# One hardware loop over the two layers of the second block, with both layers on 528 columns

## The reference, cut to what matters

```
h = concat(meta, x)                     # 16 + 512 tokens
for l in range(2):
    u    = rms_norm(h, norm1_g[l])
    z    = u @ w_in[l]                  # conv, latent attention, recurrence, 3 gates of width 1024
    a    = conv_module(z)               # causal convolution with 31 taps, layer norm
    b    = mla(z)                       # 8 heads, causal attention over 528 tokens
    c    = hgrn(z)                      # gated recurrence, 4 heads
    mix  = g0*(a@Wa) + g1*(b@Wb) + g2*(c@Wc)
    h    = h + mix @ w_out[l]
    v    = rms_norm(h, norm2_g[l])
    h    = h + relu(v @ w_ff1[l])**2 @ w_ff2[l]
return h[16:]                           # the meta tokens are dropped
```

## Time and profile before

| | |
|---|---|
| time, median of three | 2974.8 us |
| profiled execution, time | 2974.41 us |
| profiled execution, span from the first to the last instruction | 2972.6 us |
| instructions | 43610 |
| PE busy | 2765.5 us, 93% |
| DVE busy | 1307.1 us, 44% |
| ACT busy | 960.5 us, 32% |
| POOL busy | 916.2 us, 31% |
| mean granted PE clock | 0.950 of full speed |
| first layer of the second block | from 873.7 us of the span |
| second layer | from 1930.9 us of the span |

### The profile page before, as it was taken

How to read it: one execution, slowest core, us unless ns; L and a number is a source line. 1 busy time by engine, 2 the same in 40 slices (tenths; PEclk the granted TensorE clock), 3 DMA queues, 4 the chain that set the end, 5 groups by cost and what they waited for, 6 DMA issues and landing times.

```text
span 2972.6 us, 43610 instructions
## 1 busy us (share of the span) xinstructions
PE 2765.5 (93%) x16664; PEld 2397.2 (81%) x16664; DVE 1307.1 (44%) x2019; ACT 960.5 (32%) x1520; POOL 916.2 (31%) x396
## 2 busy tenths in 40 slices
PE   6999889999749989899999999989988999999999
PEld 4666768888649989788999999989887777888887
DVE  3444352223347666544353322268675443443222
ACT  3333442223322323243333322233323443333222
POOL 2111234444223312111343444434121112444444
PEclk9998779999869999999999999989999999999999
DMA  3211112222112211111122222222111101222223
GB/s 122 73 60 41 43 57 93 98 92 95 63 64 80 84 36 51 54 35 36 64 86 92 89 90 92 93 69 93 43 50 54 36 28 57 93 92 99 92 93 112
DMA packets 61678, 215.06 MB, mean 72 GB/s; under 512 B 8032, under 2 KB 8032, under 8 KB 61536
## 3 DMA queue, kind: packets, MB, share of 16 engines
q1 hardware_dynamic: 53856, 196.11, 19.1%
q10 hardware_dynamic: 7248, 15.50, 1.6%
q0 software_dynamic: 432, 1.43, 0.2%
HBM read 210.85 MB, written 2.16 MB: 72 GB/s over the span
## 4 chain that ended last, share of the span: by engine, by line
issue 68%; POOLq 32%; DMA 0%; POOL 0%; DVE 0%; DVEq 0%
POOLq L503 31%; POOLq L113 1%; POOLq L501 0%; DMA v2all<-vec 0%; POOL wl L502 0%; POOL arena L517 0%; DVE pairm L1891 0%; POOLq L515 0%; POOL fold L517 0%; POOL U L517 0%; POOLq L489 0%; POOLq L502 0%; DVE v L1895 0%; POOLq L492 0%; POOL ones L482 0%
## 5 line engine op out<-in xcount | busy, mean ns | idle before, releaser
L502 POOL TENSOR_TENSOR wl<-stage,wh 128x1024 fp32r<-128x1024 f32 x374 | 907.2, 2426 | 1988.9 <-ACT wh L1075 1988.4
L562 PE MATMUL ps<-Uh,wh 128*128 128x264 f32 (+1 forms) x2768 | 944.4, 341 | 28.8 <-DVE Ul L1597 16.5
L563 PE MATMUL ps<-Ul,wh 128*128 128x264 f32 (+1 forms) x2768 | 908.5, 328 | 0.0
L564 PE MATMUL ps<-Uh,wl 128*128 128x264 f32 (+1 forms) x2768 | 906.1, 327 | 0.0
L1075 ACT ACTIVATE wh<-stage 128x1024 fp32r<-128x1024 f32 x374 | 396.8, 1061 | 1510.7 <-PE ps L564 1508.0
L562 PEld LDWEIGHTS ps<-Uh,wh 128*128 128x128 f32 x2768 | 534.4, 193 | 113.8 <-issue 59.7
L564 PEld LDWEIGHTS ps<-Uh,wl 128*128 128x128 f32 x2768 | 532.3, 192 | 43.4
L563 PEld LDWEIGHTS ps<-Ul,wh 128*128 128x128 f32 x2768 | 535.3, 193 | 39.0 <-issue 1.9
L563 PE MATMUL ps<-HIDl,wh 128*128 128x512 f32 (+1 forms) x1024 | 347.5, 339 | 0.0
L564 PE MATMUL ps<-HIDh,wl 128*128 128x512 f32 (+1 forms) x1024 | 346.3, 338 | 0.0
L562 PE MATMUL ps<-HIDh,wh 128*128 128x512 f32 (+1 forms) x1024 | 346.2, 338 | 0.0
(11 more groups left out here) (293 smaller groups left out, 3325.5 us busy)
## 6 DMA issues: line engine op xcount, KB each, us to landing
stage<-w SPq DMA_DIRECT2D x374, 512.0 KB, 3.4
arena<-bias_rows ACTq DMA_DIRECT2D x16, 448.0 KB, 4.8
arena<-w_mla ACTq DMA_DIRECT2D x8, 384.0 KB, 3.0
H<-xT ACTq DMA_DIRECT2D x1, 2048.0 KB, 10.8
out<-H ACTq DMA_DIRECT2D x8, 256.0 KB, 2.8
arena<-pT ACTq DMA_DIRECT2D x1, 512.0 KB, 11.3
U<-pairs POOLq DMA_DIRECT2D x1, 512.0 KB, 4.5
arena<-causal POOLq DMA_DIRECT2D x1, 320.0 KB, 3.3
```

The source lines that it names most:

```text
L502: pool.tensor_tensor(wl[:, j, :], stage[:, j, :], wh[:, j, :].bitcast(F32), ALU.subtract).then_inc(w_split, 1)
L562: pe.matmul(dst, w_lead, tok.part(a_lead, h), start=(k == 0), stop=False)
L563: pe.matmul(dst, w_lead, tok.part(a_rest, h), start=False, stop=False)
L564: mm = pe.matmul(dst, w_rest, tok.part(a_lead, h), start=False, stop=(k == len(acts) - 1))
```

## The change

The Python loop over the layers becomes a hardware loop (`n.loop(LAYERS, LAYER_PER)`) on POOL, PE, ACT and DVE, around the hardware loop of the feed-forward groups that was there. A table `LOOPS["layer"]` gives what each semaphore is counted up by in one layer. As one set of instructions must serve both layers, `kept` is gone and `T2` stands in its place: the last layer also works on all 528 tokens. What is written to memory is the same, `H` without its first 16 columns.

```diff
@@ the table of increments
+    "layer": {"a_ready": 4, "cT_ready0": 22, "cT_ready1": 22, ...
+        "w_split": 136, "whole_ready": 8, "x_ready": 32, "y_ready": 8, ...},
...
-        def kept_tokens(layer):
-
-            return T2 if layer < LAYERS - 1 else T1
@@ POOL
-            for layer in range(LAYERS):
+            with n.loop(LAYERS, LAYER_PER) as layer:
@@ PE
-            for layer in range(LAYERS):
-                kept = kept_tokens(layer)
+            with n.loop(LAYERS, LAYER_PER) as layer:
...
                 split_project(U2k, T2, 1, ready=u_ready)
-                split_project(U2k, T2, 8 - 1)
-                split_project(U2k, kept, 8)
-                split_project(U2k, T2, 2 + 4)
+                split_project(U2k, T2, 8 + 8 + 2 + 4 - 1)
...
-                split_project([(mixh[:, k, :], mixl[:, k, :]) for k in range(KD)], kept, KD, ready=mix_ready)
-                feed_forward(U2k, kept, FF2_PER)
+                split_project([(mixh[:, k, :], mixl[:, k, :]) for k in range(KD)], T2, KD, ready=mix_ready)
+                feed_forward(U2k, T2, FF2_PER)
@@ and `kept` replaced by `T2` in every other place
```

More of the change, by code:

```diff
@@ L431, in program @@
         T2 = Tokens(0, T, 2)
-        def kept_tokens(layer):
-            return T2 if layer < LAYERS - 1 else T1
-        ATT_PER, FF_PER, FF2_PER = (LOOPS[x] for x in ("attention", "ff", "ff2"))
+        ATT_PER, FF_PER, FF2_PER, LAYER_PER = (LOOPS[x] for x in ("attention", "ff", "ff2", "layer"))
         def level_blocks(x, size, half):
@@ L782, in pair_products, with branch_halves, recurrence_units @@
                 mm.then_inc(pair_done[b], 1)
-            def branch_halves(acts, kept, ready=None):
+            def branch_halves(acts, ready=None):
                 tiles = split_chunk()
                 for j in range(2):
-                    yield from split_steps(tiles[4 * j:4 * j + 4], acts, kept, ready=ready if j == 0 else None)
-            def recurrence_units(kept):
+                    yield from split_steps(tiles[4 * j:4 * j + 4], acts, T2, ready=ready if j == 0 else None)
+            def recurrence_units():
                 for _ in range(4 * (HEADS_G - 1)):
@@ L794, in recurrence_units @@
                 for i in range(4):
-                    yield from branch_halves(ZAk, kept, ready=za_ready if i == 0 else None)
+                    yield from branch_halves(ZAk, ready=za_ready if i == 0 else None)
             pe.wait_ge(consts, 2)
             pe.wait_ge(consts2_in, 16 * 5)
-            for layer in range(LAYERS):
-                kept = kept_tokens(layer)
+            with n.loop(LAYERS, LAYER_PER) as layer:
                 n.next(sq_ready, KD)
@@ L833, in _ @@
                 spread_into(4, T2, 2, waits=False).then_inc(lnspread_done, 1)
-                steps = recurrence_units(kept)
+                steps = recurrence_units()
                 def fill(count):
@@ L993, in latent_units @@
                     yield from head_units(0)
-                    yield from split_steps(split_chunk(), U2k, kept)
+                    yield from split_steps(split_chunk(), U2k, T2)
                     yield from key_scales()
                     for pair in range(4):
-                        yield from split_steps(split_chunk(), U2k, kept)
+                        yield from split_steps(split_chunk(), U2k, T2)
                         tiles = split_chunk()
@@ L1325, in _ @@
                 for m in range(KD):
-                    evacuate(acc[:, m, :], kept, func=ACT.Sigmoid, split=True)
+                    evacuate(acc[:, m, :], T2, func=ACT.Sigmoid, split=True)
                 forget()
@@ L1471, in gate @@
                     b = used_up()
-                    act.activation(kept.of(gt[j]), psum_of(b, kept), ACT.Tanh, scale=0.5).then_inc(unit_free[b], 1)
+                    act.activation(T2.of(gt[j]), psum_of(b, T2), ACT.Tanh, scale=0.5).then_inc(unit_free[b], 1)
                     act.drain().then_inc(gt_ready, 1)
```

49 lines of the change are left out of this document (31 added, 18 removed), and 1 row of the table LOOPS.

## The result

| | before | after |
|---|---|---|
| time, median of 6 runs each, side by side | 2974.61 us | 3006.11 us |
| lowest and highest run | 2971.17, 2980.34 | 3001.99, 3010.38 |
| profiled execution: time, span | 2974.41, 2972.6 us | 3004.54, 3002.5 us |
| instructions | 43610 | 50303 |
| PE busy | 2765.5 us | 2792.4 us |

The changed kernel takes 1.0103 times the time of before, with a 95% interval of 1.0088 to 1.0118. That is 31.5 us by the medians and 30.1 us by the two profiled executions; the forecast was 3004 us.

What follows compares the result with a forecast made beforehand. The prediction took PE, busy 93% of the span, as the bound. Columns 24.0, registers 4 and jump 2 gave +30 us on 2974.4, so 3004 us; the 8-in-10 range was 2996 to 3017.

Steps and rivals of the forecast that it cites:

- What bounds: Whole kernel: PE, busy 93% of the span; changes count if they lengthen its work or chains it waits for.
- Columns, +24.0 (20 to 26): Last layer: 108 chunks go from 512 to 528 columns, adding 24.0 us, bounds 20 and 26.
- the marks that I took: ACT's weight-chunk starts in both layers: layer one is 24.03 us longer, with 0.39 between chunk 20 and 52.
- 108 full unit prices: Last layer: 0.24 us a unit from feed-forward groups of 92.80 and 89.00, 25.7 us if all show.
- Registers, +4 (1 to 8): Register instructions ahead of DVE's waits, 0.07 us each, in layer head, layer norm and recurrence: 2 us a layer.
- Both signs: Layer one grows by no more than 2 to 3 us; layer two equals layer one within 1 us.
- The jump, +2 (0 to 5): Step back between layers: one 3.0 us code load on ACT and DVE together, less 0.9 us of cover.
- the sign that I had named: Start of layer two: time from layer one's last tile to PE's first sum, 9.0 us, grows by 2 or 3.
- The exit at the end of the program: Program end: expected to stay the same, with the same eight DMAs of `H`; no term in the sum.
- A: Rival, recurrence and attention: DVE's register instructions set the pace, +58 us, 3032 us; chance 7 in 100.
- B: Rival, feed-forward loop: inner jumps also miss, or the long one is uncovered; +42, 3016 us; chance 8 in 100.
- C: Rival, PE's 59.7 us of weight-load idle: the loop wins back some 30 us, 2974 us; chance 5 in 100.

Runs made afterwards that it cites:

- dve_loop: 528 columns in both layers, layer loop on DVE alone, other engines written out; +34.5 us against the kernel before, ratio 1.0104.
- pe_loop: 528 columns in both layers, layer loop on PE alone, everything else written out; +24.3 us against the kernel before, ratio 1.0082.
- t2_out: The changed kernel with both layers written out again, 528 columns, no layer loop; +27.0 us against the kernel before, ratio 1.0089.
- hint: The changed kernel with a branch prefetch hint at the head of the layer loop on every engine; +35.4 us against the kernel before, ratio 1.0122.
- regs_only: t2_out with register instructions ahead of DVE's waits from layer start to the first recurrence; +26.0 us against the kernel before, ratio 1.0097.
- regs_all: t2_out with register instructions ahead of DVE's waits through both whole layers; +31.0 us against the kernel before, ratio 1.0097.
- act_loop: 528 columns in both layers, layer loop on ACT alone, everything else written out; +28.1 us against the kernel before, ratio 1.0102.

## Why the prediction was right

**What bounds.** "A change counts if it lengthens PE's own work" held: 26 of 33 us behind the first block come with the columns (PE's busy time grows by 27 us), and most of them show in windows in which PE is never idle.

**Columns, +24.0 (20 to 26).** Measured: 25.1 between the marks of layer two in the changed kernel (which includes what registers cost there), 25.8 over the groups, 27 to 30 a layer from the pair with 512 columns in both. The term is at the upper bound, nearer to the 25.7 of 108 full unit prices than to the marks that I took. The step that was off by 2 us is the comparison of layer one with layer two: I took 0.39 between chunk 20 and 52 for columns hidden behind the recurrence, but that stretch of 424 us varies by more than that between executions of the same code. In the second profile of before it took 426.4 us in both layers, where the earlier trace rows has 424.5 and 424.1. Over all profiles with constants it is 426.5 us a layer with 528 columns (nine layers, 424.5 to 428.2) and 424.2 with 512 (five layers, 421.7 to 426.4), so the 17 chunks there are worth some 2 us and not 0.39. The reason that the prediction gives for the unit price holds only in part: in proportion to the columns a group of 89.00 us would take 89.00 x 528 / 512 = 91.8. The other 1.0 of the 3.8 us comes with the second matmul and weight load for each product, which I had put at next to nothing.

**Registers, +4 (1 to 8), on DVE alone.** The layers of the looped kernels are 5.8 us longer than those of the written-out ones (2071.8 on average against 2066.1), in the range. That this is DVE's is borne out: dve_loop has it and more (2076.5), and PE pays nothing, as pe_loop is no longer than t2_out (2067.6 against 2066.9). At the seven sums the price is 0.07 us an instruction, as read from the earlier trace rows. Not shown is that registers make the rest. I had put them at handoffs of the layer norm and the recurrence; 9 of the 26 there cost nothing that could be seen. So the term has the right engine and size, and its cause is open. By the profile of the changed kernel alone the growth of layer one by 6.4 us is twice the 2 to 3 that I had asked for, and layer two then is 5.4 shorter than layer one, not equal within 1. Both signs were too strict for a kernel whose attention varies by up to 7 us.

**The jump, +2 (0 to 5).** Measured 1.1 in the gap, and 0.4 of registers. PE's first sum came 1.5 us later, where the sign that I had named was 2 or 3. The mechanism was the one expected: ACT and DVE wait for code at the same time, and PE's own load lies in its 9 us of waiting. For code, and not register work, speak the packets of instructions beside the jump (7 against 1) and the hint, with which ACT's stall is gone. ACT's stall is 2.0 us and comes behind its weight part, not beside it, as I had subtracted; the cover seems to be another one that I had not seen in the earlier trace rows: in the kernel before, DVE's first sum takes 1.1 us longer than the others and ends just behind POOL's last weight rest. The exit at the end of the program, which I had at nothing, cost 0.7 with the loop on all engines, and 0.1 or nothing with it on one.

**The rivals.** A (registers set the pace, 3032) is out: the layers are longer by 5 us with all registers, not 32. B (the inner jumps miss too, 3016) is out by the 92.80 us of the groups, and by the whole feed-forward stretch, 366.3 us in both layers. Of its rule, in the Trainium skill, page "Runtime: NRT & Kernel Launch", section "Instruction fetch mechanics", that a taken branch out of the window stalls until its code is loaded, the trace agrees for the long jump: 1.91 us on ACT, 3.25 on DVE. C (not slower) is out: of the 59.7 us in the earlier trace rows 51.5 are left in the changed kernel and in pe_loop (58.7 in t2_out), and the 7 us less did not shorten pe_loop's layers (2067.6 us, 2066.9 in t2_out).

The time was 2 us above the forecast, and the columns were larger by 2; the rest of the terms, 7 us against 6, and the first block, 4 us shorter in the profiled execution, lie within what two executions of the same code differ by. The measured difference itself is known to 26 to 35 us only, so that the forecast came within 2 us is luck; that the columns make four fifths of it is not.

## What to carry to other kernels

Rolling written-out code into a loop costs what the common body does more than the special one; here that was four fifths of the loss (26 of 33 us), and the loop's own cost (register instructions, a jump to code that was executed a millisecond earlier) was about 7 us in two thousand. Price the columns from two places of the same program that do the same work in both shapes, but take the stretch where PE never waits, at full clock, and multiply (25.7 us here, 25.8 measured); a difference of two long stretches with stalls in them is only good to some microseconds. And count what a test puts in: regs_only and regs_all had half or less of the instructions whose cost they were to show, and could not rule them out. If a kernel must be rolled, put the jump where the engine that is the bound waits anyway.

## What was not expected of the hardware

**The same code at two lengths.** The attention of layer one (chunk 44 to 52) has the same instructions in both profiles of the kernel before. These are PE's windows there, first of the one profile, then of the other (stretch, length, PE busy us, matmuls, clock, DMA share, GB/s):

```profile
1316.50:1437.50 121.00, 118.37 (x856) 0.97 0.10 36
```

```profile
1311.00:1437.60 126.60, 124.11 (x854) 0.92 0.11 34
```

The mean granted clock is 0.97 in the one and 0.92 in the other: 6.8 us and 20.5 us of the stretch lie at the lower level of 1.2 GHz. Over all profiles this stretch, with 528 columns, takes 120.7 to 127.7 us, the shortest two with 6.8 us at the lower level, the longest with 20.5 to 23.9, and most others in between; what makes the clock fall in one execution and not in another was not tested. It is about as large as the whole loop term. It is not alone: the first block, which is the same code in all fourteen profiles, ends between 890.8 us, with 143 us at the lower level, and 900.9, with 167.

**A stall that is shorter in company.** DVE's stall is 4.67 us when it jumps alone and 3.25 when all four engines jump. By the packets of the kernels with the loop on one engine, code for PE comes by q8 (118 without PE's loop, 123 with it) and code for ACT and DVE by q14 (38 without, 42 and 43 with). Why DVE's stall is the longer one alone stays open.

**DVE held up by POOL.** A DVE instruction at the head of layer two that begins while POOL splits the last chunk ends only behind it: the sum of 0.71 us takes 1.83 before and 1.90 in regs_all, the copy of 0.25 takes 1.87 in hint. In all three it is over 0.1 to 0.6 us after POOL's instruction, and where DVE comes later (after, dve_loop, act_loop) it takes its 0.71. No run took POOL's instruction away there, so this is read from the profiles, not shown.
